# A new order for the second mixer: near heads, latent heads, sparse heads, and an output product that follows them

## The reference, cut to what matters

```python
def hybrid_layer(x, pos, ...):
    x = x + 0.5 * swiglu_2(rmsnorm(x, ffn1_norm), ffn1_w_gate, ffn1_w_up, ffn1_w_down)
    h = rmsnorm(x, mix_norm) @ w_in
    (a_q, a_k, a_v, b_q, b_k, b_v, i_q, i_k, i_w, c_q, c_kv, c_kr) = split_columns(h)
    o_a = chunk_relpos_attention(hd4(a_q, 6), hd4(a_k, 6), hd4(a_v, 6), a_rel_bias)
    o_b = dsa_attention(rope(hd4(b_q, 5), pos), rope(hd4(b_k, 5), pos), hd4(b_v, 5),
                        rope(hd4(i_q, 8), pos), rope(i_k[:, :, None, :], pos)[:, :, 0, :], i_w)
    o_c = mla_attention(c_q, c_kv, c_kr, c_q_norm, c_kv_norm, c_w_uq, c_w_ukv, pos)
    x = x + jnp.concatenate([o_a, o_b, o_c], axis=-1) @ w_out
    x = x + 0.5 * swiglu_2(rmsnorm(x, ffn2_norm), ffn2_w_gate, ffn2_w_up, ffn2_w_down)
    return x
```

## Time and profile before

| | us |
|---|---|
| median of 3 runs | 1930.7 |
| lowest, highest | 1929.01, 1931.83 |
| the profiled execution, its own time | 1932.74 |
| the profiled execution, span | 1930.9 |

### The profile page before, as it was taken

How to read it: one execution, slowest core, us unless ns; L and a number is a source line. 1 busy time by engine, 2 the same in 40 slices (tenths; PEclk the granted TensorE clock), 3 DMA queues, 4 the chain that set the end, 5 groups by cost and what they waited for, 6 DMA issues and landing times.

```text
span 1930.9 us, 31579 instructions
## 1 busy us (share of the span) xinstructions
PE 1907.5 (99%) x12957; PEld 1633.8 (85%) x12957; DVE 1198.3 (62%) x2463; ACT 1011.2 (52%) x2044; POOL 92.0 (5%) x187
## 2 busy tenths in 40 slices
PE   8999999999999999999999999999999999999998
PEld 7888888988888888888888987888888888978887
DVE  5576555756655566666766745667566767545665
ACT  5565555423322555545655565556455655745554
POOL 0000001111211000010001000000000000000000
PEclk9999999999999999999999998999999999989999
DMA  6555442222202455625562332556355632324553
GB/s 234 196 220 204 170 151 97 89 73 70 92 29 73 186 188 205 239 108 179 211 219 104 120 110 96 188 177 259 113 187 201 240 117 102 137 110 156 184 187 117
DMA packets 42719, 296.16 MB, mean 153 GB/s; under 512 B 4832, under 2 KB 4960, under 8 KB 10576
## 3 DMA queue, kind: packets, MB, share of 16 engines
q1 hardware_dynamic: 41184, 288.32, 42.0%
q0 software_dynamic: 1392, 5.83, 0.8%
HBM read 293.08 MB, written 1.05 MB: 152 GB/s over the span
## 4 chain that ended last, share of the span: by engine, by line
PE 95%; DVE 2%; ACT 1%; issue 1%; POOL 1%; DMA 0%; SPq 0%; POOLq 0%; DVEq 0%; ACTq 0%
PE PS L1508 21%; PE PS L1450 16%; PE PS L1452 15%; PE PS L1451 15%; PE PS L1510 11%; PE PS L1459 3%; PE PS L1947 1%; PE PS L1742 1%; PE PS L1723 1%; PE PS L1735 1%; PE PS L1485 1%; PE PS L1859 1%; PE PS L1936 1%; PE PS L1639 1%; PE PS L1903 1%
## 5 line engine op out<-in xcount | busy, mean ns | idle before, releaser
L2335 DVE TENSOR_TENSOR wlo<-raw,whi 128x512 fp32r<-128x512 f32 (+4 forms) x780 | 616.1, 834 | 199.7 <-ACT whi L1984 193.9
L1508 PE MATMUL PS<-xhl,whi 128*128 128x512 f32 x1728 | 613.2, 399 | 0.0
L1984 ACT ACTIVATE whi<-raw 128x512 fp32r<-128x512 f32 (+4 forms) x780 | 534.5, 740 | 139.4 <-PE PS L1452 137.0
L1510 PE MATMUL PS<-xhl,wlo 128*128 128x256 f32 x1728 | 484.9, 281 | 0.0
L1508 PEld LDWEIGHTS PS<-xhl,whi 128*128 128x128 f32 x1728 | 324.7, 188 | 79.3
L1510 PEld LDWEIGHTS PS<-xhl,wlo 128*128 128x128 f32 x1728 | 326.3, 189 | 2.1
L1450 PE MATMUL PS<-whi,yh 128*128 128x512 f32 (+2 forms) x580 | 228.8, 394 | 0.3 <-DVE wlo L2335 0.2
L1452 PE MATMUL PS<-whi,yl 128*128 128x512 f32 (+2 forms) x580 | 225.0, 388 | 0.0
L1451 PE MATMUL PS<-wlo,yh 128*128 128x512 f32 (+2 forms) x580 | 224.8, 388 | 0.0
L2420 DVE TENSOR_TENSOR arena<-arena,PS 128x256 f32<-128x256 f32 x216 | 90.4, 419 | 159.2 <-ACT arena L2054 159.2
L1450 PE MATMUL PS<-whi,xhl 128*128 128x512 f32 (+4 forms) x480 | 189.0, 394 | 0.1
(11 more groups left out here) (269 smaller groups left out, 2567.2 us busy)
## 6 DMA issues: line engine op xcount, KB each, us to landing
raw<-wall SPq DMA_DIRECT2D x249, 1024.0 KB, 4.9
raw<-wall SPq DMA_DIRECT2D x12, 768.0 KB, 4.3
raw<-wall SPq DMA_DIRECT2D x8, 968.0 KB, 4.8
raw<-wall SPq DMA_DIRECT2D x4, 896.0 KB, 4.5
arena<-ebias POOLq DMA_DIRECT2D x2, 768.0 KB, 4.7
raw<-wall SPq DMA_DIRECT2D x2, 720.0 KB, 4.0
raw<-wall SPq DMA_DIRECT2D x2, 640.0 KB, 3.8
X<-x SPq DMA_DIRECT2D x2, 512.0 KB, 6.0
```

What stands on the lines that cost most here:

```text
L1508: e.matmul(b, hi[:, c0:c0 + 128], xhl[:, k, :, :].rearrange("p a t -> p (a t)"), start=(k == 0), stop=False, skip_group_check=True)
L1510: p = e.matmul(b[:, 0:256], lo[:, c0:c0 + 128], xh[:, k, :], start=False, stop=(k == 7), skip_group_check=True)
L1984: e.activation(whi[slot_of(i)][:, c].bitcast(F32R), raw[i % 3][:, c], copy).then_inc(*M.sig("whi", ("split", i, q)))
L2335: e.tensor_tensor(wlo[slot_of(i)][:, c], raw[i % 3][:, c], whi[slot_of(i)][:, c].bitcast(F32), ALU.subtract).then_inc(*M.sig("wlo", *[("ha ...
```

## The change

- The order of the input parts becomes 0, 1, 4, 5, 6, then uq and ukv, then 2 and 3. Heads run near, latent, sparse.
- The output chunks go 0, 3, then 1 and 2 by row tile. Chunk 0 waits for the near heads, chunk 3 for the latent ones, chunks 1 and 2 for the first row tile, then the second row tile, of the sparse heads. The next stage's two lead chunks are split after all four.
- `turn_out` is done by row tile, in a chain of its own (`outs`).
- `rest` is changed on the way: 0.5, from part 5 on 1, after the last part 9.
- Near heads get score buffers of their own, six in the memory of BQK; the sparse turns wait for the near heads (mark `near`). DG, the weights of the index sum, moves from AQK to CQK, so that `turn_c` waits for both index sums. `Space` is laid out anew.
- In the planner a split no longer moves the time at which the following step is due. This and the table touch stage 1 as well.
- `BLANKS`: 12 in stage 5, 14 in stage 8, 245 in stage 1 at partly other steps, 27 in stage 4.

```diff
@@ plan
-            out += parts[1] + parts[2] + [(l, "uq", 0, 1440), (l, "ukv", 0, 1280)]
-            for j in (3, 4, 5, 6):
+            for j in (1, 4, 5, 6):
                 out += parts[j]
-            out += [(l, "wout2", 2, 2048), (l, "wout2", 3, 2048), "lead0"]
-            out += [(l, "wout2", 1, 2048), "lead1", (l, "wout2", 0, 2048)]
+            out += [(l, "uq", 0, 1440), (l, "ukv", 0, 1280)] + parts[2] + parts[3]
+            out += [(l, "wout2", j, 2048) for j in (0, 3, 1, 2)] + ["lead0", "lead1"]
@@ BLANKS
...
+    ('wo', 1, 2, 0, 0): 5, ('wo', 1, 2, 1, 0): 2, ('proj', 4, 'gh', 0, 0): 27, ('turn_x', 5, 0, 0): 6,
+    ('latent_up', 5, 'uq', 0, 0): 6, ('turn_x', 8, 0, 0): 6, ('u_turn', 8, 'a', 0, 0): 2,
+    ('latent_up', 8, 'uq', 0, 0): 6,
@@ do
+        ready = self.ready
         for eng, us in PACE.get(step[0], ()):
-            self.now[eng] = max(self.now[eng], self.ready) + us
-            self.ready = self.now[eng] + HOP
+            self.now[eng] = max(self.now[eng], ready) + us
+            ready = self.now[eng] + HOP
+        if step[0] != "split":
+            self.ready = ready
@@ mix2, unit
+            S = self.slots["N" if kind == "a" else "S", s]
...
+            while kind == "a" and 6 not in made:
+                yield 1
...
             self.do("u_out", s, kind, h, tt)
+            self.pump()
@@ mix2, latent
+            while ("sum", 1) not in made:
+                yield 1
             for j in range(5):
                 yield from self.room(1)
                 self.turn(("tc", s, j), "turn_c", s, j)
@@ mix2, sparse
+            while not {("a", 0), ("a", 1)} <= heads:
+                yield 1
+            self.mark("near", s)
             for j in range(3):
                 yield from self.room(1)
                 self.turn(("tb", s, j), "turn_b", s, j)
@@ mix2, products
-            for j in (1, 2):
+            for j in (1, 4, 5, 6):
                 yield from proj(j)
+                if j == 5:
+                    self.rest = 1
...
-            for j in (3, 4, 5, 6):
+            for j in (2, 3):
                 yield from proj(j)
...
+            self.rest = 9
+            while "out a" not in made:
+                yield 1
             yield from self.room(4)
             self.acc(s, "wout2")
...
+            down = self.down("wout2", s, lambda j: (l, "wout2", j), [0, 3], False)
+            while next(down) is None:
+                yield 1
+            while "out c" not in made:
+                yield 1
+            yield from down
+            js = (1, 2)
+            while "out b0" not in made:
+                yield 1
+            ids = [self.take(l, "wout2", j) for j in js]
+            for _ in self.tail_row(s, "wout2", "wout2", js, ids, 0):
+                self.pump()
+                yield 1
+            while "out b1" not in made:
+                yield 1
+            for n, _ in enumerate(self.tail_row(s, "wout2", "wout2", js, ids, 1)):
+                self.pump()
+                if n == 1:
+                    self.turn_half(s + 1, 0)
+            self.used.update(ids)
+
+        def outs():
+            for kind, ks, tts in (("a", (0,), (0, 1)), ("c", (6,), (0, 1)), ("b0", (2, 4), (0,)), ("b1", (2, 4), (1,))):
+                while not {(kind[0], tt) for tt in tts} <= heads:
+                    yield 1
+                if kind == "c":
+                    self.mark("lead", s)
+                    self.lead_from = ("lead", s)
+                for k0 in ks:
+                    for tt in tts:
+                        yield from self.room(1)
+                        self.turn(("ot", s, k0, tt), "turn_out", s, k0, tt)
+                yield 1
+                made.add("out " + kind)
...
-        units = [unit(kind, h, tt, n) for kind, n in (("c", 5), ("b", 5), ("a", 6)) for tt in range(2) for h in range(n)]
-        self.woven(products(), 0.5, index(), latent(), sparse(), near(), *units)
+        units = [unit(kind, h, tt, n) for kind, n in (("a", 6), ("c", 5), ("b", 5)) for tt in range(2) for h in range(n)]
+        self.woven(products(), .5, outs(), index(), latent(), sparse(), near(), *units)
@@ build, layout
-        BQK, CQK = sp.take(3, 2, 256), sp.take(5, 2, 256)
+        AQK, EB = sp.take(3, 2, 256), sp.take(6, 256)
+        DG = [arena[:, sp.at + 1024 * i:sp.at + 1024 + 1024 * i].rearrange("p (j k) -> p j k", k=128)
+              for i in range(2)]
+        CQK, VC = sp.take(5, 2, 256), sp.take(2, 5, 65)
+        BQK, VB = sp.take(3, 2, 256), sp.take(2, 5, 65)
...
+        ubuf += [BQK[:, i // 2, i % 2, :] for i in range(6)]
```

More of the change, by code:

```diff
@@ L595, in down, with tail_row @@
             yield True
+    def tail_row(self, s, acc, name, js, ids, tt):
+        for n, (j, i) in enumerate(zip(js, ids)):
+            end = n == len(js) - 1
+            for nn in range(2):
+                for kk in range(2):
+                    stop = end and kk == 1
+                    sig = [(name, s, "end", tt, nn)] if stop else []
+                    if (tt, nn, kk) == (1, 1, 1):
+                        sig.append(("use", i))
+                    self.do(name, s, j, kk, tt, (nn,), i, False, stop, sig)
+                if end:
+                    self.do("resid", s, acc, name, tt, nn)
+                    self.bank.give((acc, s, 2 * tt + nn))
+                    self.do("sumsq", s + 1, tt, nn)
+                yield 1
+        self.do("scale", s + 1, tt)
     def tail(self, s, acc, name, key, js):
@@ L1067, in sparse @@
         def sparse():
-            for j, first in ((2, "uq"), (3, 3)):
-                while first not in made:
+            for j in (2, 3):
+                while j not in made:
                     yield 1
@@ L1106, in products @@
                 made.add(nm)
-            for j in (3, 4, 5, 6):
+            for j in (2, 3):
                 yield from proj(j)
-            while not {("b", 1), ("c", 1)} <= heads:
+            self.rest = 9
+            while "out a" not in made:
                 yield 1
-            for k0 in (4, 6):
-                self.turn(("ot", s, k0), "turn_out", s, k0)
-            self.mark("lead", s)
-            self.lead_from = ("lead", s)
             yield from self.room(4)
             self.acc(s, "wout2")
-            yield from self.down("wout2", s, lambda j: (l, "wout2", j), [2, 3], False)
@@ L1118, in products @@
-            while ("a", 1) not in heads:
+            down = self.down("wout2", s, lambda j: (l, "wout2", j), [0, 3], False)
+            while next(down) is None:
                 yield 1
-            for k0 in (2, 0):
-                self.turn(("ot", s, k0), "turn_out", s, k0)
-            self.tail(s, "wout2", "wout2", lambda j: (l, "wout2", j), (1, 0))
-        units = [unit(kind, h, tt, n) for kind, n in (("c", 5), ("b", 5), ("a", 6)) for tt in range(2) for h in range(n)]
-        self.woven(products(), 0.5, index(), latent(), sparse(), near(), *units)
+            while "out c" not in made:
+                yield 1
@@ L2800, in scores @@
                 prev = before(("st", s), u)
-                for t in due(("pe", (tile,)), unit_free(s, "S", u), prev and ("act", ("exp", s) + prev), *toks):
+                for t in due(("pe", (tile,)), *unit_free(s, "N" if u[0] == "a" else "S", u), prev and ("act", ("exp", s) + prev), *toks):
                     e.wait_ge(*t)
@@ L2825, in u_norm, with turn_out @@
                     *M.sig("dve", ("o", s, kind, tt), ("free", ("pv", s, kind, tt))))
-            def turn_out(s, k):
-                low(xh, xl, k, 8, ("ot", s, k), ("oh", s, k), ("ol", s, k))
+            def turn_out(s, k, tt):
+                tile, c = ("ot", s, k, tt), slice(tt * 128, (tt + 1) * 128)
+                for t in due(("act", ("oh", s, k, tt))):
+                    e.wait_ge(*t)
+                e.tensor_tensor(xl[:, k:k + 2, c], bank(tile)[:, 0:256].rearrange("p (k t) -> p k t", k=2),
+                                xh[:, k:k + 2, c].bitcast(F32), ALU.subtract).then_inc(
+                    *M.sig("dve", ("ol", s, k, tt), ("free", tile)))
             def final(s, tt):
```

76 lines of the change are left out of this document (40 added, 36 removed).

## The result

The changed kernel takes **1909.8 us** (median of four runs, 1906.81 to 1914.93); the kernel before took 1931.26 us beside it (four runs, 1929.01 to 1933.24). The ratio is 0.9888, 95% interval 0.987 to 0.9906: 1.1% faster. The forecast was 1897 us with a range of 1887 to 1912. The range held, the number is 12.8 us too low; one of the four runs, at 1914.93 us, lies above the range. The profiled execution of the changed kernel is its fastest run, 1906.81 us, with a span of 1905.0 us (before: 1930.9).

A forecast was written before the change was run, and what follows sets the result against it. TensorE was taken as the bound, 99% busy, with blanks hiding waits and some low clock in the second mixers. Gains of 41.5 us less 8 of new waits gave 33.5 us, so 1897 us, range 1887 to 1912.

The forecast's parts named there:

- The blanks and what they covered: Second mixers: blanks fall from 114 to 6 and 112 to 8, real work replacing them; gains 15.5 and 14.3 us.
- The low clock: Second mixers: the half-rate stretches of 10.3 and 10.2 us go; gains 3.4 and 4.2 us if the clock holds.
- The end of the stage: Last part of each second mixer: new waits around the sparse heads cost 4 us a stage, bounds 0 and 10.
- my first rival: End of each second mixer stays uncovered, DVE and ACT at some 90%: 9 us a stage, 1907 us, chance 0.12.
- Small parts: turn_out by row tile, tail_row, the new buffer layout and the weight stream: 0 us, layout bound a few us.
- The first mixer: Stage 1: order and blanks move under the new split rule; taken as 0, bounds -5 and +5 us.
- the clock: Second mixers: a half-rate interval returns elsewhere in each stage, 5.1 us each, 1907 us; chance 0.10.
- the first mixer gets worse: Stage 1 loses its 5 us bound through the new order: 1902 us; chance 0.08.
- The sum: Whole kernel: 41.5 us gained less 8 of new waits is 33.5; span 1897.4 us, median 1897.2.
- the uncovered end: Ends of the second mixers: sparse chain as late as the near one was, 9 us a stage, 1907 us; chance 0.12.
- the low clock in the second mixers: Rival: a half-rate interval comes at another place in each second mixer, 5.1 us each, 1907 us; chance 0.10.

The follow-up runs named there:

- Experiment 5: The kernel before, in its old order, with the new short table of blanks for stages 5 and 8: 1940.41 us, ratio 1.0037.
- tile_both: m1_old with the sparse heads' output pairs 2 and 4 turned for both row tiles together: 1899.68 us, ratio 0.9836.
- m1_blank: The changed kernel, new order kept, with the old blanks in stage 1: 1923.7 us, lowest 1917.7, highest 1933.0.
- pump_more: m1_old with two lead-chunk splits instead of one listed at each pair of blocks in a second mixer's last tail row: 1900.06 us, ratio 0.9829.
- rest1_only: m1_old without the value 9 of `rest` after the last part, the 1 from part 5 on kept: 1908.79 us, ratio 0.9877.
- m1_old: The changed kernel with the old split rule and old blanks in stage 1: 1898.71 us, ratio 0.9822; run again, 1898.9 us.
- m1_rule: The changed kernel with the old split rule, so the old order, in stage 1, new blanks kept: 1907.5 us.
- m1_new: The kernel before with only stage 1 changed (new split rule and new blanks there): 1936.26 us, ratio 1.0035.

## Why the prediction was right, and where it was off

- *The blanks and what they covered* (15.5 + 14.3 us): right. L1518 has 298 matmuls in the span, 6 and 8 in the stages; their loads take 0.78 and 1.07 us. Experiment 5 shows that this was a gain only because of the order: the same cut without it costs 0.4%.
- *The low clock* (3.4 + 4.2): right for the second mixers, at 1.00 all through.
- *The end of the stage* (4 us of new waits each, bounds 0 and 10): right in sign, nearly twice too large. By my sum a stage without new waits would take 168.8 - 21.6 + 0.7 = 147.9 us and 168.4 - 21.3 + 0.7 = 147.8; it takes 149.9 and 150.1, so they are worth 2.0 and 2.3 us. The idle time is 1.7 us, of it 0.7 the wait that stayed; I had said 3 to 5. The working behind it was off in several places. From the end of part 3 to the first sparse score I counted a bare chain of 4.8 us, with a wait of 3.4 if the latent heads were through. It takes 11.1 us, and PE is busy for 10.47 of them: the latent heads are far from through, and the chain hides behind them. The case with no wait was nearly the true one (0.6 us). Nor does the idle time lie between part 3 and the last heads for the most part: half of it, 0.85 us, is behind them (0.7 of that is the old wait). DVE and ACT have 26.0 and 26.5 us in this last part, near the 29 that I had estimated, but the part is 43.9 us long, and PE has 42.2 us of work in it where I had said about 32. So they were busy for 60% there and not near their limit, and the 90% of my first rival was wrong. For the ten sparse units I took 2 us from loads that were busy for 80%. The loads are busy for 78% now (12.68 of 16.3 us) and PE is idle for 0.3 us: that share was no measure of waiting, and the row was not of sparse units alone, as said above.
- *Small parts*: right, by tile_both.
- *The first mixer* (0, bounds -5 and +5): this is the term that failed, and the one whose row I had named as the test (442 us; it took 450.6). I took 5.2 us of idle PE as the size that an order can move and said nothing of the clock there. But the price of one 2.1 us wait was the low clock behind it. My rival "the clock" had the right mechanism and the wrong stage; "the first mixer gets worse" had the right stage, a chance of 0.08, and 5 us in place of 8.7 in the profiled run and 11.1 between the medians. Where it came true the clause of the Trainium skill that I had weighed against the second mixer applied: "TensorE: Matmul & The Clock Gate", section "HAM oscillation — how this bites in real kernels", says that idle stretches bring the half rate back, and tells it of waits longer than the ones here. The trace agrees for the wait of 2.1 us (13.6 us at 0.50) and for its filling (none). The 1.7 us of idle time of each second mixer, in pieces of 0.7 us at most, brought no fall. But no wait is needed: one fall in m1_blank came after 8.3 us in which PE was never idle.
- *Stages 6 and 9*: +1.4 and +1.7 us, which I had not foreseen. I had the next stage's two chunks "split after all four, so they no longer stand before a score" and counted it as a gain alone. What is late next is the split itself, and behind it, by pump_more, the scaled rows: a stage that ends 18 us sooner brings its tail's work on ScalarE and VectorE into less time. That last reason is argued, not tested by itself; it fits that rest1_only, whose stages end 5.6 us later, has no such loss.
- *The sum*: without the first mixer's part it was good. m1_old has a span of 1897.3 us and a median of 1898.7, where I had 1897.4 and 1897.2: 37 us gained in the second mixers for 33.5 forecast, and 3 us lost in stages 6 and 9. That these two errors cancel is luck. So is part of the range: I had stretched it to 1912 for two rivals, the uncovered end and the low clock in the second mixers, of which neither came about, and what filled it was the first mixer, 11 us where I allowed 5.

The version to keep of those that ran is m1_old: 1898.7 and 1898.9 us, 0.6% under the changed kernel and 1.7% under the one before (0.9822 [0.9807, 0.9838]).

## What to carry to other kernels

- Where matmuls without a reader fill waits, count them as waits, and ask of each run what would be done in its place. Taking them out pays only behind an order that removes the wait; here the order and the cut together gained 37 us in the two stages, and the cut alone made the kernel 0.4% slower, which by the rows of experiment 5 is the price of the low clock that came with it.
- An edit to the planner reaches every stage that it plans. A table tuned by hand to one order is part of that order: when a rule moves the steps, compare all stages by length, and keep the old rule where its table was made for it.
- The cost of a wait on TensorE is not its length alone but also what the clock does behind it. If the lowest and highest run of a kernel lie 8 us apart where a variant of it has 1.6, look for a stretch at 0.50 and for the last wait ahead of it. Not every fall has one (m1_blank, 368.3 us).

## What the runs showed of the hardware

- After a wait of 2.1 us at 545.1 us in stage 1 the granted clock was 0.50 for 13.6 us in one kernel and for 30.7 us in another with the same list there. PE was busy all through both stretches (13.60 of 13.60 and 30.70 of 30.70 us), so being busy did not end them at once.
- Falls came behind shorter waits too: behind 1.01 us in m1_blank (13.7 us at 0.50), and in m1_rule at 428.6 us, 0.2 us into a wait of 2.43 us, with 0.67 us of idle time shortly ahead. One came with none: in m1_blank PE was busy from 360 to 368.3 us, from 364.9 on with matmuls of 64 rows and ones of 2 columns, and the clock was 0.51 for the next 3.4 us.
- A clock that has fallen can be a matter of the run: m1_old and pump_more have the same steps and the same waits before 553 us, the last of 0.8 us, and only in pump_more it fell, for 6.8 us. m1_new has ten runs in groups at 1931 to 1933, 1935 to 1942 and 1948 to 1949 us.
- The length of a fall was from 3.4 (rest1_only, behind a 2.6 us wait) to 30.7 us. What decides it was not settled by these runs.
